# Attention stages: the copies of turned probabilities are put ahead of the next exponentials, and GpSimd scales the first halves

## What is computed

```
s = einsum('bnqkgd,bnskd->bnkgqs', qb, kc) * scale - slopes * dist   # masked
p = softmax(concatenate([s, sink], -1))[..., :-1]
o = einsum('bnkgqs,bnskd->bnqkgd', p, vc)
```

```
s = einsum('bqhd,bkhd->bhqk', qn, k_nope) + einsum('bqhd,bkd->bhqk', qr, k_rot)
p = masked_softmax(s * scale, key <= query)
o = einsum('bhqk,bkhd->bqhd', p, v)
o_nsa = g[..., 0:1] * o_cmp + g[..., 1:2] * o_slc + g[..., 2:3] * o_win
```

## Time and profile before

| what | us |
|---|---|
| median of the runs (lowest, highest) | 2273.97 (2273.53, 2280.85) |
| profiled execution, its own time | 2270.7 |
| its span | 2268.7 |
| stage "wa" in the span | about 162 to 218.6 |
| stage "ca" in the span | about 2055 to 2208.5 |
| PE busy over the span | 1933.6 (85%) |
| VectorE busy | 1517.4 (67%) |
| ScalarE busy | 519.0 (23%) |
| GpSimd busy | 849.2 (37%) |
| mean granted TensorE clock | 0.928 of full |

### The profile page before, as it was taken

How to read it: one execution, slowest core, us unless ns; L and a number is a source line. 1 busy time by engine, 2 the same in 40 slices (tenths; PEclk the granted TensorE clock), 3 DMA queues, 4 the chain that set the end, 5 groups by cost and what they waited for, 6 DMA issues and landing times. The chain is left out here.

```text
span 2268.7 us, 24638 instructions
## 1 busy us (share of the span) xinstructions
PE 1933.6 (85%) x8290; PEld 1326.6 (58%) x8290; DVE 1517.4 (67%) x3147; ACT 519.0 (23%) x1206; POOL 849.2 (37%) x638
## 2 busy tenths in 40 slices
PE   5997789959887979988899889888896659998987
PEld 3874568748656856655555555555552237754555
DVE  5468745468987966776666666666667778436654
ACT  3344122122135820010000000000000032336541
POOL 3430034333231044555555454555556613320002
PEclk8998589979979989999999999999998979999989
DMA  7987979676485589999999999999999932201002
GB/s 282 356 324 255 315 279 388 222 293 232 158 301 193 207 340 405 406 406 406 406 406 407 408 406 406 405 406 406 406 406 403 389 116 90 75 19 38 1 1 74
DMA packets 187404, 648.95 MB, mean 286 GB/s; under 512 B 19601, under 2 KB 36113, under 8 KB 186001
## 3 DMA queue, kind: packets, MB, share of 16 engines
q1 hardware_dynamic: 101888, 336.45, 39.0%
q0 software_dynamic: 73728, 268.47, 29.9%
q10 hardware_dynamic: 11664, 42.47, 5.4%
HBM read 561.33 MB, written 85.98 MB: 285 GB/s over the span
## 5 line engine op out<-in xcount | busy, mean ns | idle before, releaser
L1775 PE MATMUL ps<-arena 128*128 128x512 f32 x1024 | 499.1, 633 | 132.3 <-DVE arena L1612 112.8
L1623 DVE CUSTOM_DVE_ANT_0 arena<-arena 128x1024 bf16<-128x1024 f32 x256 | 313.8, 1226 | 279.4 <-DMA arena<-u_rows,u_row 162.9
L1764 PE MATMUL ps<-rows_n,arena 128*128 128x256 f32 x2048 | 468.7, 380 | 0.6 <-DMA arena<-in_u 0.6
L1764 PEld LDWEIGHTS ps<-rows_n,arena 128*128 128x128 f32 x2048 | 387.5, 191 | 100.0 <-issue 53.3
L1775 PEld LDWEIGHTS ps<-arena 128*128 128x128 f32 x1024 | 197.3, 200 | 379.8 <-issue 220.7
L1406 POOL DMA_INDIRECT arena<-u_rows,u_row x256 | 293.5, 1146 | 202.7 <-DMA gates<-arena 122.4
L1406 POOL DMA_INDIRECT arena<-in_v,expert x192 | 201.5, 1049 | 314.0 <-DVE arena L1644 296.0
L1644 DVE SCALAR_TENSOR_TENSOR arena<-arena,wt 128x1024 f32<-128x1024 f32 x192 | 245.7, 1280 | 0.4
L1739 ACT ACTIVATE ge<-dots 128x2 f32<-128x2 f32 x128 | 26.2, 205 | 903.7 <-DVE dots L1623 903.7
L192 DVE STREAM_TRANSPOSE tdst<-tsrc 128x1024 f32<-128x1024 f32 x128 | 155.3, 1230 | 86.8 <-DMA tsrc<-in_u 40.8
L237 POOL TENSOR_TENSOR in_wlo<-in_raw,in_whi 128x1024 fp32r<-128x1024 f32 x45 | 114.2, 2539 | 226.6 <-ACT in_whi L233 226.6
(11 more groups left out here) (444 smaller groups left out, 2780.9 us busy)
## 6 DMA issues: line engine op xcount, KB each, us to landing
tsrc<-in_u SPq DMA_DIRECT2D x128, 512.0 KB, 7.7
u_rows<-tdst SPq DMA_DIRECT2D x128, 512.0 KB, 6.3
arena<-in_u SPq DMA_DIRECT2D x128, 512.0 KB, 7.6
arena<-in_v SPq DMA_DIRECT2D x128, 512.0 KB, 7.6
in_raw<-in_panels ACTq DMA_DIRECT2D x37, 512.0 KB, 3.7
gates<-arena SPq DMA_DIRECT2D x8, 2048.0 KB, 8.7
arena<-gates SPq DMA_DIRECT2D x16, 1024.0 KB, 18.6
mg_raw<-in_panels ACTq DMA_DIRECT2D x28, 512.0 KB, 6.7
```

What stands on the lines that cost most here:

```text
L1623: nc.vector.tensor_tensor_reduce(out=junk[:, n % 2], in0=u_slot[n % NU], in1=hrows[:, n // NPICK], scale=1.0, scalar=0.0, op0=ALU.mult, op ...
L1764: mm = nc.tensor.matmul(ps[:, j % 2, 0:TD], ud[:, j % RJ, k], rows_n2[:, 0, k], start=k == 0, stop=k == KD - 1)
L1775: mm = nc.tensor.matmul(ps[:, 4 + 2 * t + c], park[:, j % NPK, t * P:(t + 1) * P], vd[:, j % RJ, c * T:(c + 1) * T], start=j == 0, stop=j ...
```

## The change

Each part, in the order of the diff:

- `prob` gets four buffers instead of three (`RPB`).
- GpSimd runs a loop over all pairs: it waits for `scale_ready` and scales half 0 of each pair in place. VectorE scales half 1 only. `scale_ready` is raised by the reciprocal, or by the gate product where there is one. In "ca", `make_lo` comes after that loop on GpSimd.
- turn and values move one step back on PE: step p is now scores(p), turn(p-3), values(p-4). turn waits for GpSimd's semaphore for half 0, and VectorE's for half 1.
- On ScalarE step p is now copy(p-4), exps(p). `make_hi` stays behind exps in steps 24 and 25.
- VectorE empties a unit one step later.
- exps(p) waits for both scalings of pair p-4, a wait more than before.

```
-        NB, RPB, RPT = 2, 3, 3
+        NB, RPB, RPT = 2, 4, 3
...
-            if ahead is not None:
-                @block.gpsimd
-                def _(pool):
+            def scaled(eng, p, h):
+                pr = prob[:, p % RPB, h, 0:pairs[p]["n"]]
+                return eng.tensor_scalar(pr, pr, rs[:, p % 4, 2, h:h + 1], None, ALU.mult)
+
+            @block.gpsimd
+            def _(pool):
+                for p in range(n):
+                    pool.wait_ge(scale_ready, p + 1)
+                    scaled(nc.gpsimd, p, 0).then_inc(prob_pool, 1)
+                if ahead is not None:
                     for i in range(2):
                         ahead.make_lo(pool, i)
...
-                        pe.wait_ge(prob_ready, j + 1)
+                        pe.wait_ge((prob_pool, prob_ready)[h], p + 1)
...
-                for p in range(n + 3):
+                for p in range(n + 4):
                     if p < n:
                         scores(p)
-                    if 2 <= p < n + 2:
-                        turn(p - 2)
-                    if p >= 3:
-                        values(p - 3)
+                    if 3 <= p < n + 3:
+                        turn(p - 3)
+                    if p >= 4:
+                        values(p - 4)
...
-                    chain(nc.vector.reciprocal(r[:, 2], r[:, 0]))
+                    ins = nc.vector.reciprocal(r[:, 2], r[:, 0])
                     if x["gate"] is not None:
-                        chain(nc.vector.tensor_tensor(r[:, 2], r[:, 2], x["gate"], ALU.mult))
-                    for h in range(2):
-                        pr = prob[:, p % RPB, h, 0:x["n"]]
-                        nc.vector.tensor_scalar(pr, pr, r[:, 2, h:h + 1], None, ALU.mult).then_inc(prob_ready, 1)
+                        chain(ins)
+                        ins = nc.vector.tensor_tensor(r[:, 2], r[:, 2], x["gate"], ALU.mult)
+                    ins.then_inc(scale_ready, 1)
+                    v.wait_ge(scale_ready, p + 1)
+                    scaled(nc.vector, p, 1).then_inc(prob_ready, 1)
...
-                    if done < len(units) and last_pair[done] <= p - 4:
+                    if done < len(units) and last_pair[done] <= p - 5:
...
                     if p >= 4:
-                        act.wait_ge(prob_ready, 2 * (p - 4) + 2)
+                        act.wait_ge(prob_ready, p - 3)
+                        act.wait_ge(prob_pool, p - 3)
...
-                for p in range(n + 2):
+                for p in range(n + 4):
+                    if p >= 4:
+                        copy(p - 4)
                     if p < n:
                         exps(p)
-                    if p >= 2:
-                        copy(p - 2)
```

More of the change, by code:

```diff
@@ L524, in attention_stage @@
             rs = sb(st, name + "_rs", [P, 4, 3, 2])
-            names = ["scores", "negmax", "expd", "prob", "turned", "copied", "pv", "unit_out", "dve", "eighth_made"]
-            scores_ready, negmax_ready, exp_ready, prob_ready, turned, copied, pv_done, unit_out, dve, eighth_made = sems(
+            names = ["scores", "negmax", "expd", "prob", "turned", "copied", "pv", "unit_out", "dve", "eighth_made", "scale", "prob_pool"]
+            scores_ready, negmax_ready, exp_ready, prob_ready, turned, copied, pv_done, unit_out, dve, eighth_made, scale_ready, prob_pool = sems(
                 st, " ".join(f"{name}_{x}" for x in names))
@@ L629, in _ @@
                 done = 0
-                for p in range(n + 4):
+                for p in range(n + 5):
                     if p < n:
```

## The result

| | median (lowest, highest), us | ratio to before, 95% interval |
|---|---|---|
| before, 5 runs | 2278.15 (2273.53, 2280.85) | |
| after, 5 runs | 2264.08 (2260.48, 2266.68) | 0.9946 (0.9927 to 0.9965) |

The changed kernel is 0.54% faster, 12.3 us by the ratio. By the bound of 0.3% that is faster. The forecast had "same" at 0.66 and 2271.0 as its time; the result lies within the range (2261 to 2279), where the rival of the clock had put it (2264). That it meets 2264 to a tenth is luck: the forecast counted from 2273.97, the median of three runs, and before now has 2278.15 in five. As differences, the forecast had 2.9 us less, the rival about 10, and the runs show 12.3.

What follows compares the result with a forecast made beforehand. "wa" leans on VectorE, "ca" on PE, neither quite full. "wa" -3.7, 0.5 given back next, "ca" +0.3: together -2.9 from the profiled 2270.7, plus 3.3 to the runs' median, 2271.0 us; 8-in-10 range 2261 to 2279.

Steps and rivals of the forecast that it cites:

- the rival of the clock: PE, mostly "ca": shorter waits keep its clock up, saving 5.5 us, plus 1.5 in "wa"; 2264 us, chance 0.24.
- The listing of the order: ScalarE: one copy stands between two exponentials in both orders, so PE's 16.8 us wait for it in "ca" stays in kind.
- The seven waits without a compressed product: PE in "ca", gated part and first latent scores: each wait ahead of a turn shrinks by 0.43, together 3.0 us less.
- The four places with it: PE in "ca": compressed product moves behind the wait, +0.57 each, minus a later wait of 0.41; together +0.6 us.
- The turn of 128: PE in "ca": it must wait for both halves of a copy of 512, 0.2 in eight gated rounds, +1.6 us.
- ScalarE's two conversions: For the next stage, between exponentials and the next copy; one stands in full ahead of a turn, +1.1 us (0 to 2.2).
- booked with -3.7: "wa": -2.7 for one scaling less in ten VectorE steps, -1.0 net for the last output behind the last finish.
- The bound 1.71: GpSimd's scaling takes at most 1.71 us for 512 columns, 0.85 for 256, taken from a two-input subtraction; hidden, costing nothing.
- the rival of GpSimd first: VectorE's scaling waits for GpSimd's in every pair, slowing "wa" and holding unit outputs in "ca"; +7.1, 2281 us, chance 0.14.
- The cover of 7.8 us: End of "ca": GpSimd's last scaling and two subtractions, 6.4 us, fit into 7.8; without it, an output could be held 2.35.
- the +1.0 for a pipeline one step longer: End of "ca": one turn and values more after the last exponentials, about +1.0 us (bounds 0 and 2).
- the four cases: Own forecast 0.46, clock kept up 0.24, nothing gained by VectorE's share (2274.6 us) 0.16, GpSimd ahead of VectorE 0.14.

Runs made afterwards that it cites:

- e5: The changed kernel with a useless ScalarE copy of 512 columns behind every exponentials of 512 (12 in "ca"); 2277.21 us, ratio 1.0002 to before.
- e3: The changed kernel with ScalarE's copy moved one step, copy(p-3) instead of copy(p-4) ahead of exps(p); 2239.48 us, ratio 0.9844 to before.
- e7: The kernel before with two ScalarE lines swapped, copy(p-2) ahead of exps(p), no deeper pipeline, no GpSimd scaling; 2259.78 us, ratio 0.9927 to before.
- e2: The changed kernel with the old order on all engines, leaving GpSimd's half of the scaling and the fourth prob buffer; 2280.69 us, ratio 1.0015 to before.
- e1: The changed kernel with both scalings back on VectorE, leaving only the later turn; 2266.93 us, ratio 0.9954 to before.
- e6: The changed kernel with a useless ScalarE copy of 128 columns behind every exponentials of 512 (12 in "ca"); 2267.78 us, ratio 0.9958 to before.
- e4: The kernel of e3 with both halves scaled by VectorE instead of sharing with GpSimd; 2246.14 us, ratio 0.9857 to before.

## Why the prediction was right in range and wrong in its case

**What failed: "My sum takes it to stay, as waits of 1.2 us stay."** The waits did stay, but the clock did not. It moved by 0.07 in "ca", and a move beyond 0.05 was one of the prediction's own signs of being wrong. The term had the value 0, and PE's matmuls came out 8.4 us shorter in "ca" (132.30 - 123.93). The clock alone is somewhat more: the stretched rows of PE's timeline, each against the same group of matmuls at full clock, add up to some 10.9 us in before and 1.6 in after, 9.3 less (my estimate from the rows); turns of 128 that wait inside took 0.9 back. In before, PE's matmuls are stretched behind waits of 1.48, of 0.71 and 0.59 in a row, of 1.60 to 1.61 three times, and of 2.36, but not behind its 1.72, 1.47 and 1.36; in after only once, in the filling of the pipeline behind 1.62. In after, its other waits, most of them 0.86 to 1.17 and one of 1.81 at the end, were followed by no such stretch. The two spare copies show the direction of cause: they add nothing but delay on ScalarE, and the stretched matmuls come back with it, clearly in e5. I had the rival, and priced it at "something under half" of the 12.4 us that the mean clock leaves missing; it was two thirds to three quarters. In "wa" it gave nothing (39.83 to 39.30 us of PE, clock 0.82 to 0.81), where the rival had 1.5.

**The listing of the order was right.** One copy stands between two exponentials in both orders, and the waits for it stayed in kind: 14 of them, 13.4 us (forecast: near 15). e3 and e7 show it from the other side. As soon as the copy passes the exponentials, these waits are gone (one of 1.0 us is left in e3, none in e7).

**The sizes beside each other.** 0.43 less in each latent wait was priced; it was 1.61 - 1.06 = 0.55. The rest of it is the copy's first half, which now has 128 columns instead of 256: 0.28 against 0.41 us for one half. The seven waits without a compressed product fell from 10.9 to 6.3 us in all, 4.5 where 3.0 was priced. The four places with it were really three and the filling. The three waited 0.72, 0.47 and 0.59 and now 0.86, 0.86 and 1.17, where 1.3 had been expected; the wait two turns later, counted four times, was there twice (0.41 and 0.42); in the filling 0.98 grew to 1.62. Together that is +0.9 for the +0.6 of the sum. The turn of 128, which waits for both halves of a copy of 512, is stretched from 0.39 to 0.70 in five gated rounds and not eight (5 x 0.31 = 1.6 us, the sum's own 1.6). But this time is taken off the wait behind it, which ends with ScalarE and not with PE: behind such a turn of 0.70 the wait is 0.86, and behind the one that took 0.39 (at 2130.74) it is 1.17, just 0.31 more. So the sum counted it twice. ScalarE's two conversions, booked with +1.1, cost nothing that shows: around them PE waited 1.04 us before (0.33 and 0.71, for scaling) and 0.76 after. In all, PE's idle time fell by 2.8 us. The two kinds of waits fell by 3.4 + 0.8 = 4.2, so 1.4 of other small idle came in; 0.8 of it is waits for exponentials in the filling (0.60 and 0.16).

**"wa"** was booked with -3.7 and measured 56.55 - 53.03 = 3.5. The sum is right within the scatter of 0.9, its two terms are less sure: alone, GpSimd's half gives 2.7 as priced and the later turn 2.2 instead of 1.0, and they overlap. The 0.5 given back in the next stage can't be told from the 9 us by which the unchanged code differs between profiles.

**GpSimd's price.** The bound 1.71 was no bound: the scaling of 512 took 1.91 and that of 256 took 1.08 instead of at most 0.85. A row with two inputs is no ceiling for one with a single input and a scalar for each partition. The Trainium skill (GPSIMD Engine Reference, Elementwise, side-by-side cycle accounting) would have made it 769 ns; the measurement is 2.5 times that. It cost PE one wait of 0.2 us, since the extra step hides it, as predicted; e2 shows what it costs without that cover.

**Who comes first.** VectorE did, as taken. One release in after, VectorE's timeline:

```profile
2121.16 0.42 DVE L543 TENSOR_SCALAR ca_prob<-ca_prob,ca_rs 128x384 f32<-128x384 f32 x1
```

and GpSimd's:

```profile
2121.22 3.46 POOL L543 TENSOR_SCALAR ca_prob<-ca_prob,ca_rs 128x384 f32<-128x384 f32 x2 [2.34 <-DVE ca_rs L627]
```

GpSimd starts 0.06 later (its row of 3.46 joins two scalings), and VectorE's 0.42 is the usual time for 384 columns. VectorE's scalings kept their time in the mean of each size (0.49 at 512 columns, 0.48 before), so the rival of GpSimd first did not occur. With both subtractions at the end, the gate product no longer shares its time with them: mean 161 ns, and none of 1.86 us as before.

**The ends.** The cover of 7.8 us for the subtractions was nearly enough. VectorE's last rows in "ca" after, answering to the last of the earlier trace rows:

```profile
2198.80 0.84 DVE L2274 CAST act_hi<-zz 128x512 fp32r<-128x512 f32 x1
2199.68 0.69 DVE L2275 TENSOR_TENSOR act_lo<-zz,act_hi 128x512 fp32r<-128x512 f32 x1
```

GpSimd's subtractions ran from 2194.54 for 4.82 us, to 2199.36. The cast took 0.84 instead of the 0.43 of the others, 0.4 us of the stage. From the last scores of 512 to the end it was 13.08 us before and is 12.89, so the +1.0 for a pipeline one step longer seems not to show. It did come: before has 1.5 us of stretched matmuls in that piece (turns and values behind the wait of 2.36) and after has none. Where both are stretched, before and e1, it is 13.08 and 13.87, 0.8 more.

**The chances.** The shares given for the four cases add up to some 0.23 for faster and 0.07 for slower, not 0.25 and 0.09. Faster is what came, mostly by the clock.

## What to carry to other kernels

Write out the order of every engine before and after a reordering, and ask which instruction the waiting engine's release stands behind: a copy that has to be early must pass the long instruction ahead of it in its own queue, and making everything one step older doesn't do that (e7 gains by two swapped lines what the whole change gains). Where PE idles once in a round and the matmuls behind it are stretched, price the wait with the clock: in e5 one us more of it cost two. Judge a change by the sum of the stages that it touches, cut at the same instructions, and the total by the runs; a single profile's span moved by 9 us in code that had not changed.

## What the runs showed of the hardware

- GpSimd's in-place product with one scalar for each partition took 0.69, 1.08, 1.47 and 1.91 us for 128, 256, 384 and 512 columns of float32; VectorE took 0.29, 0.35, 0.42 and 0.49 for the same.
- In "ca" of these profiles single waits of PE for the copy up to 1.26 us were followed by matmuls at 1.2 GHz in one case (e1, behind 0.86 at 2090.97), besides two short ones in a row in before (0.71 and 0.59); e6 has three of 1.26 without it. Behind waits of 1.38 to 1.81 they were sometimes stretched and sometimes not, in one kernel and at the same place of the round. In e2 and e4 the stage's third scores, behind a wait of 0.56 for exponentials, took 1.60 and 1.65 us instead of 0.92; in the other seven profiles they did not.
- A VectorE cast of 0.43 us took 0.84, 1.26 and 0.66 when it began under GpSimd's two-input subtraction (after, e3, e6), and ended 0.28 or 0.29 us after the subtraction each time. Gate products of 0.16 us took 1.3 to 1.9 under a subtraction (six, in before, e1, e4 and e7) and ended 0.01 to 0.03 after it. The Trainium skill (SBUF — State Buffer, Who interferes with whom) has the port held for a whole instruction; these rows agree.
- GpSimd's scaling held a cast in one place and not in another: in e2 seven casts that began under a scaling of 384 columns took 0.75 or 0.76 us, and in after seven casts inside a row of two scalings (384 and 512 columns) took the usual 0.43, though GpSimd had begun first there too. By the rule just named they should have been held as well; why they were not stays open.
- With the same instructions in the same order, 1840 us between the two stages differed by up to 9 us between profiles, and the 53 us of "wa" by 0.9.
